# A decoder layer on one core: x normalised first, the memory chunks moved between the attention heads, and mask, scale and maximum of the scores in one VectorE instruction per block

## The reference, cut to what matters

```
h = rmsnorm(x); z = h @ w_in     # columns: pool | q (16 heads) | k | v (2 kv heads) | memory q | gates
A = causal pooling over windows 2, 4, 8, 16, then a 128x128 map per group
B = attention over a window of 128 tokens, rotary q and k, with a sink per head:
    s = where(mask, (q @ k.T) * 64**-0.5, -1e30);  m = max(max(s), sink)
    p = exp(s - m) / (sum(exp(s - m)) + exp(sink - m));  o = p @ v
C = attention of 4 heads of 128 into 256 memory tokens: kv = rmsnorm(mem) @ w_mem_kv
x = x + (g0 * (A @ wA) + g1 * (B @ wB) + g2 * (C @ wC)) @ w_out
h2 = rmsnorm(x); queries, top 16 of product keys, softmax gates
x = x + gates applied to gelu(h2 @ u) @ v, over 16384 experts (done densely, weighted by gates)
out = rmsnorm(x)
```

## Time and profile before

| | |
|---|---|
| median of 3 runs | 2134.08 us (2133.06 to 2134.82) |
| the profiled execution, its own time | 2133.81 us |
| its span, first to last instruction | 2132.0 us |
| granted TensorE clock, mean | 0.991 |
| PE busy | 2071.6 us, 97% |
| DVE, ACT, POOL busy | 1226.4, 792.1, 849.2 us |

### The profile page before, as it was taken

The page is one execution under the profiler, slowest core; times in us unless marked ns, Lnnn a source line. Parts: engine busy times, 40 slices in busy tenths (PEclk is TensorE's granted clock), DMA queues, the critical chain, the costliest instruction groups (busy, mean ns, idle before and its releaser), DMA issues.

```text
span 2132.0 us, 30302 instructions
## 1 busy us (share of the span) xinstructions
PE 2071.6 (97%) x10616; PEld 1708.8 (80%) x10616; DVE 1226.4 (58%) x1851; ACT 792.1 (37%) x1136; POOL 849.2 (40%) x361
## 2 busy tenths in 40 slices
PE   6988899999999999999999999999999999999998
PEld 5766788887888888888888888888888888888886
DVE  6678321112129999777777777025555555555556
ACT  5566522323223222344554455332222222222223
POOL 4411144443335444433333333444444444444443
PEclk9999999999999999999999999999999999999999
DMA  5211022222224444446556556665555555565552
GB/s 207 89 40 40 30 99 96 92 97 89 78 79 133 148 138 147 143 118 191 189 196 197 188 191 197 212 222 219 179 182 196 217 184 179 183 224 189 184 182 102
DMA packets 108516, 323.47 MB, mean 152 GB/s; under 512 B 11200, under 2 KB 11200, under 8 KB 106304
## 3 DMA queue, kind: packets, MB, share of 16 engines
q1 hardware_dynamic: 108192, 322.49, 44.9%
q10 hardware_dynamic: 288, 0.54, 0.1%
HBM read 253.78 MB, written 69.21 MB: 151 GB/s over the span
## 4 chain that ended last, share of the span: by engine, by line
issue 47%; PE 32%; POOL 19%; DMA 1%; POOLq 0%; DVE 0%; SPq 0%; ACT 0%
PE bank L637 32%; POOL w_lo L417 19%; DMA a_in<-a_rows 0%; POOLq L416 0%; DVE x_sb L1384 0%; DMA a_rows<-abuf 0%; POOLq L420 0%; DVE x_sb L1379 0%; DVE wf L1358 0%; POOL mask L401 0%; POOL mask L403 0%; SPq L266 0%; DVE wT_lo L1362 0%; ACT wT_hi L994 0%; POOL mask L398 0%
## 5 line engine op out<-in xcount | busy, mean ns | idle before, releaser
L417 POOL TENSOR_TENSOR w_lo<-raw,w_hi 128x1024 fp32r<-128x1024 f32 x346 | 845.5, 2444 | 1264.1 <-ACT w_hi L763 1264.1
L763 ACT ACTIVATE w_hi<-raw 128x1024 fp32r<-128x1024 f32 x346 | 366.7, 1060 | 1216.5 <-PE bank L440 698.7
L440 PE MATMUL bank<-hT_hi,w_hi 128*128 128x512 f32 x1488 | 590.9, 397 | 0.5 <-POOL w_lo L417 0.4
L440 PE MATMUL bank<-hT_hi,w_lo 128*128 128x512 f32 x1488 | 580.5, 390 | 0.0
L440 PE MATMUL bank<-hT_lo,w_hi 128*128 128x512 f32 x1488 | 579.3, 389 | 0.0
L1362 DVE TENSOR_TENSOR wT_lo<-wf,wT_hi 128x512 fp32r<-128x512 f32 x128 | 313.5, 2449 | 131.0 <-ACT wT_hi L994 131.0
L440 PEld LDWEIGHTS bank<-hT_hi,w_lo 128*128 128x128 f32 x1488 | 279.4, 188 | 59.9
L440 PEld LDWEIGHTS bank<-hT_hi,w_hi 128*128 128x128 f32 x1488 | 279.8, 188 | 58.7 <-issue 3.9
L440 PEld LDWEIGHTS bank<-hT_lo,w_hi 128*128 128x128 f32 x1488 | 280.1, 188 | 56.1 <-issue 0.7
L637 PE MATMUL bank<-w_hi,wT_hi 128*128 128x512 f32 x1024 | 315.3, 389 | 0.1
L637 PE MATMUL bank<-w_lo,wT_hi 128*128 128x512 f32 x1024 | 315.3, 389 | 0.0
(11 more groups left out here) (217 smaller groups left out, 1518.9 us busy)
## 6 DMA issues: line engine op xcount, KB each, us to landing
raw<-stream SPq DMA_DIRECT2D x346, 512.0 KB, 3.4
a_rows<-abuf SPq DMA_DIRECT2D x128, 256.0 KB, 4.0
g_rows<-gstage SPq DMA_DIRECT2D x32, 1024.0 KB, 6.2
g_in<-g_rows SPq DMA_DIRECT2D x16, 2048.0 KB, 9.3
a_in<-a_rows SPq DMA_DIRECT2D x128, 256.0 KB, 3.5
x_sb<-x SPq DMA_DIRECT2D x4, 512.0 KB, 8.5
out<-x_sb SPq DMA_DIRECT2D x4, 512.0 KB, 2.6
subkeys<-subkeys SPq DMA_DIRECT2D x1, 1024.0 KB, 14.5
```

Of the source, the lines that this page charges most:

```text
L417: pool.tensor_tensor(w_lo[:, k % 2, :], raw[:, k % RAW, :], w_hi[:, k % 2, :].bitcast(f32), ALU.subtract).then_inc(lo_ready, 1)
L440: last = pe.matmul(dst, w[:, slot, k * P:(k + 1) * P], rhs[low][:, r0 + k - k0, :], start=(k == k0 and wi == 0), stop=(k == k1 - 1 and wi ...
L763: act.activation(w_hi[:, base % 2, :], raw[:, slot, :], ACT.Copy).then_inc(hi_ready, 1)
```

## The change

Four things are done.

- Order of the stream. k, v, the four pooling chunks and two q chunks come first (chunks 0 to 7). The eight memory chunks are now all of one kind (256 columns, 24 matmuls); `S_MEM` gives their numbers, 8, 10, ... 22, each between two q chunks `S_Q`. Chunks from 26 on keep their places. The values among them come out transposed (`vmT`) and are turned by two transposes each.
- x goes first at the head: x is loaded, normalised in place and transposed into all eight banks. VectorE takes two of the four sums of squares. `mem` follows; its transposes (`turn_mem`) stand between the pooling chunks. `memT` lies where x lay, and x is loaded again (4 x 512 KB) before it is needed for the sum.
- A memory chunk in each head pair (`memory_filler`): pair 0 has it after its scores, the others inside `window_values`, after the second block of transposes.
- Mask, scale, maximum and sink: one `tensor_tensor_reduce` per block of 128x256, eight per pair, in place of four masks, four maxima and one `scalar_tensor_tensor`. The exponentials take scale 1.0.

Besides, GpSimd does the subtractions of the first 24 chunks in four pieces each.

```diff
-S_KM, S_VM, S_K, S_V, S_POOL = 0, 4, 8, 9, 10
-S_Q, S_QM, S_GATE = 14, 22, 26
+S_K, S_V, S_POOL, S_GATE = 0, 1, 2, 26
+S_Q = (6, 7, 9, 11, 13, 15, 17, 19, 21, 23, 24, 25)
+S_MEM = (8, 10, 12, 14, 16, 18, 20, 22)
...
-            def low(n, k):
+            def low(n, k, pieces=1):
                 pool.wait_ge(hi_ready, n + 1)
-                pool.tensor_tensor(w_lo[:, k % 2, :], raw[:, k % RAW, :], w_hi[:, k % 2, :].bitcast(f32),
-                                   ALU.subtract).then_inc(lo_ready, 1)
+                for at in range(0, D, D // pieces):
+                    cols = slice(at, at + D // pieces)
+                    last = pool.tensor_tensor(w_lo[:, k % 2, cols], raw[:, k % RAW, cols],
+                                              w_hi[:, k % 2, cols].bitcast(f32), ALU.subtract)
+                last.then_inc(lo_ready, 1)
...
+            def project(n, rhs, b, read, cols=T, before=None, used=True):
 
                 chunk(n)
+                if read:
+                    pe.wait_ge(proj_read, read)
+                product(bank[b][:, 0:cols], n % 2, rhs, before=before, used=used)
...
+            def memory_filler(u):
+
+                n = S_MEM[u]
+                turns = 1 <= u <= 4
+                project(n, memT, 0, n, cols=M, used=not turns)
+                if turns:
+                    for m in range(MT):
+                        last = pe.transpose(bank[0][:, M + m * P:M + (m + 1) * P], vmT[:, m * P:(m + 1) * P],
+                                            ident[:, :])
+                    last.then_inc(chunk_used, 1)
+
+            def window_values(u, filler=None):
...
                     if n == 0 and u >= 1:
                         pe.wait_ge(y_lo, 4 + u)
+                    if n == 1 and filler is not None:
+                        memory_filler(filler)
                     if n >= 1:
                         pe.wait_ge(probT_read, 4 * u + n)
...
                 if u >= 1:
-                    window_values(u - 1)
-                project(S_Q + u + 2, R_Q + u + 2, hT, strict=(u > 0))
+                    window_values(u - 1, filler=u)
+                else:
+                    memory_filler(0)
+                project(S_Q[u + 2], hT, 0, S_Q[u + 2])
...
             for u in range(8):
+                split(S_Q[u + 1] + 2)
                 next_q(u)
                 if u >= 1:
-                    turn_probs(TT, 4 * (u - 1))
+                    turn_probs(TT, 4 * (u - 1), which=(0, 1))
+                filler_out(u)
+                if u >= 1:
+                    turn_probs(TT, 4 * (u - 1), which=(2, 3))
                     outputs_high(8 + u - 1, u)
+                split(S_MEM[u] + 2)
                 act.wait_ge(capped, u + 1)
...
+                turned_q = (2 + u, S_Q[u + 1] % 2 if u == 0 else 0, qr[:, (u + 1) % 2, :])
+                if u == 0:
+                    rotate_bank(*turned_q)
                 if u >= 2:
                     dve.wait_ge(probT_done, 4 * (u - 1))
                 for b in range(4):
                     j, h = b // 2, b % 2
                     dve.wait_ge(scored, 4 * u + b + 1)
...
+                    for n in (2 * j, 2 * j + 1):
+                        last = dve.tensor_tensor_reduce(
+                            out=pr[:, n, h, :], in0=bank[2 + 2 * h + j][:, n % 2 * 2 * WINDOW:(n % 2 + 1) * 2 * WINDOW],
+                            in1=mask[:, min(n, 1), :], scale=HEAD ** -0.5, scalar=sinks[:, 2 * u + h:2 * u + h + 1],
+                            op0=ALU.add, op1=ALU.max, accum_out=mcap[:, 2 * n + h:2 * n + h + 1])
+                    last.then_inc(score_read, 1)
+                if 0 < u < 7:
+                    rotate_bank(*turned_q)
```

More of the change, by code:

```diff
@@ L283, in _ @@
             first_u = S_U + AHEAD
-            with sp.Fori(RAW, first_u // RAW * RAW - RAW + 1, RAW) as n0:
+            with sp.Fori(RAW, S_GATE + 6 - RAW + 1, RAW) as n0:
+                for k in range(RAW):
+                    load(n0 + k, k)
+            sp.wait_ge(chunk_used, S_MEM[-1] + 1)
+            for t in range(TT):
+                load_x(t)
+            with sp.Fori(S_GATE + 6, first_u // RAW * RAW - RAW + 1, RAW) as n0:
                 for k in range(RAW):
@@ L448, in _, with turn @@
             yT = (yT_hi, yT_lo)
-            def project(n, rn, rhs, cols=T, strict=False, before=None):
+            def project(n, rhs, b, read, cols=T, before=None, used=True):
                 chunk(n)
[L453 to L462, removed]
+                if read:
+                    pe.wait_ge(proj_read, read)
+                product(bank[b][:, 0:cols], n % 2, rhs, before=before, used=used)
+            def turn(src, tok_ready, base, k):
+                pe.wait_ge(turned_lo, base + max(k - 3, 0))
                 for t in range(TT):
@@ L484, in _ @@
[L484 to L499, removed]
@@ L500, in _, with turn_mem @@
-            turn(xn, MT + 1, KC, KC - 1, first=True)
-            project(S_K, R_K, hT, before=split_ready(KC))
-            project(S_V, R_V, hT)
+                                        x_sb[:, t, k * P:(k + 1) * P], ident[:, :])
+                    if t == TT - 1:
+                        last.then_inc(turned, 1)
+            project(S_K, hT, 0, 0, before=split_ready(0))
+            project(S_V, hT, 1, 0)
+            def turn_mem():
+                pe.wait_ge(normed, TT + MT)
+                for k in range(KC):
+                    for t in range(MT):
+                        at = k % 2 * M + t * P
+                        last = pe.transpose(bank[2 + k // 2][:, at:at + P],
+                                            mem_sb[:, t, k * P:(k + 1) * P], ident[:, :])
+                    last.then_inc(turned, 1)
@@ L907, in _ @@
                 if u == 0:
+                    split(S_Q[9] + 2)
                     next_q(8)
@@ L1066, in _ @@
                 dve.wait_ge(angles, made + 1)
+            dve.wait_ge(std_ready, 1 + TT)
+            step(dve.reciprocal(rstd[:, 0:MT], std[:, 0:MT]))
+            for t in range(MT):
+                normalise(mem_sb, mem_sb, t, t)
             dve.wait_ge(consts, 2)
@@ L1126, in _ @@
                 window(gi)
+                if gi == 2:
+                    for k in range(KC):
+                        mem_low(k)
                 if gi >= 1:
                     mix_low(gi - 1)
-            rotate(1, R_Q, qr[:, 0, :])
+            rotate_bank(1, S_Q[0] % 2, qr[:, 0, :])
+            dve.wait_ge(proj_read, S_Q[0] + 1)
+            rotate(qr[:, 0, :])
             mix_low(3)
```

314 lines of the change are left out of this document (160 added, 154 removed).

## The result

| | before | after |
|---|---|---|
| median | 2134.03 us (2133.06 to 2134.82, 4 runs) | 2156.86 us (2153.41 to 2159.72, 4 runs) |
| profiled execution, its own time | 2133.81 us | 2155.82 us |
| span | 2132.0 us | 2153.8 us |

The ratio is 1.0108, 95% interval 1.0092 to 1.0123: 23 us slower, where 25 were forecast. The windows by stage come first, with the columns of the earlier trace rows. The five stages are the head up to the first scores, pair 0, pairs 1 to 6, pair 7, and the memory heads up to the gates.

The account below looks back on a forecast made before the run. VectorE and ScalarE together were taken to set the 14.8 us pair cycle. 68.9 + 16.0 + 143.0 + 14.9 + 40.15 = 283.0 to the gates, 25 us later than before: 2159 us, range 2144 to 2174.

Parts of the forecast that it names:

- The wait: Pairs 1 to 6: TensorE waits about 7 us before the memory chunk for VectorE's q bank read; window and exponentials queue behind.
- Rival 4: Pairs: bank read before TensorE needs it, so no memory-chunk wait; 15.2 us per pair, 2107 us in all; chance 0.07.
- The pair term by term: Pairs 1 to 6: one serial chain from `den` to `den`, 23.9 us (23.7 in pairs 5 and 6), six making 143.0.
- the block: VectorE's fused instruction in the pairs: 0.51 us each, ends 0.41 and 0.67, so 4.1 us for eight.
- The clock: Memory chunk in pairs: after the wait TensorE runs 4.8 us at half clock, making chunk and transposes 5.1 us.
- Rival 1: Pairs 1 to 6: the clock does not fall during the wait; 2.0 us less per pair, 2147 us; chance 0.11.
- Quarters: GpSimd's four-piece subtractions in the pairs: met four times, so `den` to the end of normalising stays 4.64 us, ends 2.7 and 5.3.
- Rival 2: Pairs: quarters let VectorE through, normalising takes 2.7 + 0.2 us; 1.8 less in seven pairs, 2146 us; chance 0.10.
- the head's term: Head: TensorE waits for the first pooling window behind VectorE's rotary angles; 3.1 us, between 0 and 8.
- Rival 3: Pairs costlier: blocks at 0.67 us (2168), or clock low through the rest of the window (2170); chance 0.12.
- The other stages: Outside pairs 1 to 6: k near 16, first scores 68.9, pair 0 16.0, pair 7 14.9, memory heads 40.15 us.

Follow-up runs that it names:

- experiment 1: Changed kernel with VectorE reading the q bank ahead of the eight blocks in pairs 1 to 6: 2127.47 us, 29.4 less than the changed kernel.
- experiment 5: Changed kernel with the q bank read ahead and the memory chunk of pairs 1 to 7 behind the window, its copy and split behind the exponentials: 2115.34 us.
- experiment 6: Changed kernel with 22 unused matmuls ahead of the memory chunk in pairs 1 to 6 to keep TensorE busy: 2144.97 us.
- experiment 7: Kernel before with only GpSimd's subtractions of the first 24 chunks cut into four pieces: 2123.62 us, ratio 0.9964.
- experiment 3: Changed kernel with GpSimd's subtractions whole, not in quarters, in the first 24 chunks: 2159.38 us.
- experiment 8: Kernel before with the fused instruction and GpSimd's quarters together, old order of the stream: 2114.02 us, ratio 0.9913.
- experiment 4: Kernel before with the fused instruction alone, eight blocks and then the q bank read: 2119.41 us, ratio 0.9935.
- experiment 2: Changed kernel with the old four masks, four maxima and one small instruction in place of the eight fused blocks: 2167.43 us.
- experiment 10: The version of experiment 5 with unused matmuls added in TensorE's waits before the first pooling window and pair 0's memory chunk: 2110.54 us.

## Why the prediction was right, step by step

**The wait.** Shown. It stood where it was forecast, ended by the read of the q bank, 5.7 us in each of six pairs ("about 7", of which the shorter blocks account for 0.9), with ScalarE waiting 9.95 for the chunk (9) and VectorE 8.66 + 4.29 in all (12), and moving that one read gave back 29 us (experiment 1). Rival 4, that the wait isn't there, is out for the changed kernel. Its price of 15.2 us per pair holds for another kernel: experiment 5 has 15.6 on average.

**The pair term by term.** From `den` at 131.01 to `den` at 154.53:

| step | predicted | measured | mean of the six pairs |
|---|---|---|---|
| `den` to the end of normalising | 4.64 | 4.48 | 4.44 |
| eight blocks | 4.1 | 3.24 | 3.24 |
| bank read and semaphore | 0.7 | 0.83 | 0.83 |
| memory chunk and transposes | 5.1 | 5.76 | 5.23 |
| rest of the window | 3.6 | 3.6 | 3.61 |
| output copy and split | 1.6 | 1.44 | 1.44 |
| exponentials | 4.2 | 4.17 | 4.17 |
| sum | 23.9 | 23.5 | 22.96 |

Over six pairs the mean is 22.96, against 23.8 forecast: 5.2 us less in all. The mis-sized term is the block; the other differences cancel. I took 0.51 for a block, between 0.41 and 0.67, for fear of the accumulator's read; that read is hidden, and the lower end was right at 0.405. The estimate from the Trainium skill (VectorE: DVE Perf Modes, "The TRN2 errata"), 0.42 us each and 3.4 for the eight, was nearer than mine: the trace has 3.24. The memory chunk is right only on average: it took from 4.3 us (pair 5) to 5.8 (pair 4), by how much of it the low clock covered.

**The clock.** Rival 1 is out. The granted clock fell to 0.50 in each of the six pairs, over the whole chunk in pairs 3 (shown) and 4 and over part of it in the others, and keeping TensorE busy took 2.0 us off a pair on average (experiment 6), just what rival 1 had given as its price. What the prediction held for rival 1, that a wait of 1.29 us did nothing visible, was read in one pair. The 0.92 of pairs 1 to 6 in the earlier trace rows hides falls to 0.50 in pairs 1, 3 and 5 of the kernel before, behind waits of 2.1 to 2.2 us; the six pairs took 14.8 to 15.0 us all the same.

**Quarters.** Rival 2 is out in the changed kernel: normalising took 4.12 where 4.64 less the `den` work, 4.2, was kept, and the kernel before had 4.29 with whole subtractions. So the stretch hardly shrank for being cut into four. But quarters help at the head, where the angles took 13.4 us for the instructions that took 19.8 before (20.8 in the prediction, with the pooling counts behind them), and in the old order the pairs as well (experiment 7). I had put the head's term (3.1 for the wait for the first window) between 0 and 8; it was 2.99, and 4.36 with whole subtractions (experiment 3).

**Rival 3** is out in both its forms: the blocks started 0.405 apart, and the clock was back at 1.00 in the rest of the window.

**The other stages.** k at 14.82 (16), first scores at 69.09 (68.9), pair 0 16.2 (16), pair 7 14.7 (14.9), memory heads 41.1 (40.15, with a clock of 0.96 now). 69.1 + 16.2 + 137.8 + 14.7 + 41.1 = 278.9, where 283.0 was forecast. The agreement at the first scores is in part luck: k came 1.2 us sooner than I had it, and it doesn't show there.

**What the change was worth, part by part.** The fused instruction alone gives 13.7 us and the quarters alone 10.4, and 19.3 together, in the old order. The new order with its chunk inside the window turns that into a loss of 23, and with the chunk behind the window it costs and brings nothing.

## What to carry to other kernels

Work put into an engine's gap must be free to start when the gap opens. The gap here lay ahead of the chunk's bank being read, so the chunk didn't fill a wait but made a longer one, with the window and the exponentials queued behind it; look at what the added work itself waits for, and at what stands behind it in the queue. And once TensorE sets the stage, moving its work from the head into the pairs was no gain here (experiments 5 and 8), while two VectorE savings that each bring the stage down to what TensorE needs with its wait for ScalarE don't add.

## What the runs showed of the hardware

- The tensor_tensor_reduce of 128x256 from PSUM with its maximum costs 0.405 us from one start to the next, the read of its accumulator (76 ns) nothing.
- Normalising, which reads and writes SBUF, is stretched by GpSimd's subtraction from 2.19 us to 4.29 for eight instructions (both in experiment 4); masks and blocks out of PSUM are not (2.47 and 0.405 with or without it). The Trainium skill, SBUF — State Buffer, "Who interferes with whom", says that a VectorE instruction with at most one SBUF input outside the fast modes does not contend with GpSimd; the masks agree. Normalising reads one SBUF tensor too, and undisturbed its instructions start some 0.26 us apart (2.19 for eight), where a block of the same size takes 0.405; whether it runs in such a mode no run here tests.
- A wait of TensorE of 3.0 us ahead of the first pooling window left the clock at 1.00 in two executions of the changed kernel and took it to 0.50 in experiments 1, 2, 5 and 6, whose head is the same list. These rows are of the changed kernel and then of experiment 5:

```profile
41.10:45.00 3.90, 3.90 (x25) 3.16 (x24) 2.27 (x4) 2.78 (x5) 1.24 (x2) 1.00 0.33 126
```

```profile
41.10:45.00 3.90, 3.63 (x11) 2.50 (x12) 0.99 (x4) 1.67 (x3) 0.00 (x0) 0.50 0.36 134
```

In these four the first scores come 2.3 to 3.6 us later than in the changed kernel. The length of the wait alone doesn't decide it. k started at 14.82 and 14.83 where the clock stayed and at 15.11 to 15.64 where it fell; whether that decides it stays open. With added matmuls in the wait the clock stayed at 1.00 (experiment 10), but k started at 14.97 there, so that alone doesn't show that they kept it. The Trainium skill, TensorE: Matmul & The Clock Gate, "Part 1: The HAM clock gate", says that the slow stretch at the start varies between runs of one kernel. The two traces of the changed kernel don't show that, and the mean clocks of the seven executions of experiment 1 (0.989 to 0.995) do show a difference between executions of one program.
